# Sliding attention: outputs by feature and turned back, or by query at once

## The reference

```
s = einsum('bcqhgd,bckhd->bchgqk', qc, kb) * (HEAD_DIM ** -0.5)
s = where(kmask, s + bias, -inf)
p = softmax(concatenate([s, sink], axis=-1), axis=-1)[..., :-1]
o = einsum('bchgqk,bckhd->bcqhgd', p, vb)
```

## Time and profile before

| | us |
|---|---|
| median of 3 runs | 2401.78 |
| the runs | 2395.17, 2401.78, 2403.42 |
| span of the profiled execution, first to last instruction | 2401.4 |
| TensorE busy, records | 2179.5 (91%), 11296 |
| VectorE busy | 1648.4 (69%) |
| ScalarE busy | 1486.0 (62%) |

### The profile page before, as it was taken

The page is one execution under the profiler, slowest core; times in us unless marked ns, Lnnn a source line. Parts: engine busy times, 40 slices in busy tenths (PEclk is TensorE's granted clock), DMA queues, the critical chain, the costliest instruction groups (busy, mean ns, idle before and its releaser), DMA issues. The chain is left out here.

```text
span 2401.4 us, 35987 instructions
## 1 busy us (share of the span) xinstructions
PE 2179.5 (91%) x11296; PEld 1794.5 (75%) x11296; DVE 1648.4 (69%) x3068; ACT 1486.0 (62%) x2262; POOL 467.5 (19%) x529
## 2 busy tenths in 40 slices
PE   6999999879789999999899984999999999999980
PEld 5788888756477877877678873778888888788860
DVE  5323231267587777777733346999999999999976
ACT  4323241276587777777633331878887888788867
POOL 0111111143122222221000001222222222122221
PEclk9999999979989999999899995999999999999995
DMA  6535352543441222222233325997887969998838
GB/s 202 175 116 181 114 185 86 154 91 93 114 109 51 58 71 69 64 69 77 56 122 140 141 95 184 350 370 238 298 266 228 299 199 364 317 299 300 266 91 301
DMA packets 220554, 420.62 MB, mean 175 GB/s; under 512 B 47912, under 2 KB 97144, under 8 KB 219288
## 3 DMA queue, kind: packets, MB, share of 16 engines
q1 hardware_dynamic: 187760, 316.08, 39.1%
q0 software_dynamic: 31648, 101.89, 14.7%
q10 hardware_dynamic: 1040, 1.31, 0.2%
HBM read 437.68 MB, written 86.39 MB: 218 GB/s over the span
## 5 line engine op out<-in xcount | busy, mean ns | idle before, releaser
L2533 DVE TENSOR_TENSOR moe_w_lo<-fetch_w_raw,moe_w_hi 128x1024 fp32r<-128x1024 f32 x376 | 435.2, 1217 | 8.8 <-ACT moe_w_hi L2462 8.6
L2462 ACT ACTIVATE moe_w_hi<-fetch_w_raw 128x1024 fp32r<-128x1024 f32 x376 | 368.8, 1053 | 60.6 <-PEq L96 27.9
L2587 PE MATMUL moe_ps_gu<-moe_w_hi,moe_xT_hi 128*128 128x512 f32 x736 | 294.1, 400 | 4.0 <-DVE moe_xT_lo L2544 4.0
L2589 PE MATMUL moe_ps_gu<-moe_w_hi,moe_xT_lo 128*128 128x512 f32 x736 | 289.3, 393 | 0.0
L2588 PE MATMUL moe_ps_gu<-moe_w_lo,moe_xT_hi 128*128 128x512 f32 x736 | 289.1, 393 | 0.0
L1495 ACT ACTIVATE fox_p_hi<-fox_ps_t 128x512 fp32r<-128x512 f32 (+4 forms) x352 | 182.4, 533 | 102.2 <-PE fox_ps_t L1635 100.6
L1562 DVE TENSOR_TENSOR fox_p_lo<-fox_ps_t,fox_p_hi 128x512 fp32r<-128x512 f32 (+4 forms) x352 | 211.6, 613 | 47.4 <-ACT fox_p_hi L1495 45.6
L2539 DVE TENSOR_TENSOR moe_d_lo<-fetch_d_raw,moe_d_hi 128x1024 fp32r<-128x1024 f32 x184 | 213.1, 1220 | 10.9 <-ACT moe_d_hi L2470 10.9
L1635 PE MATMUL fox_ps_t<-ident,fox_s 128*128 128x128 f32 (+1 forms) x1216 | 198.1, 278 | 18.2 <-ACT fox_s L1488 17.9
L1549 DVE CUSTOM_DVE_ANT_0 fox_s<-fox_ps_r,fox_ncum 128x512 f32<-128x512 f32 (+4 forms) x352 | 191.7, 570 | 22.9 <-PE fox_ps_r L1620 16.0
L511 ACT ACTIVATE proj_qk_out<-proj_ps_chunk 128x512 f32<-128x512 f32 x52 | 31.1, 598 | 261.7 <-PE proj_ps_chunk L744 261.7
(11 more groups left out here) (346 smaller groups left out, 5061.1 us busy)
## 6 DMA issues: line engine op xcount, KB each, us to landing
fetch_w_raw<-in_w_e_gate_dram SPq DMA_DIRECT2D x192, 512.0 KB
fetch_w_raw<-in_w_e_up_dram SPq DMA_DIRECT2D x192, 512.0 KB
fetch_d_raw<-in_w_e_down_dram SPq DMA_DIRECT2D x92, 1024.0 KB
ahead_raw<-in_w_in_dram SPq DMA_DIRECT2D x24, 1024.0 KB, 5.2
gates_wide<-in_x_dram SPq DMA_DIRECT2D x16, 512.0 KB
h<-gates_wide POOLq DMA_DIRECT2D x16, 512.0 KB, 3.3
gates_wide<-qT SPq DMA_DIRECT2D x32, 256.0 KB, 4.4
mix_h<-h SPq DMA_DIRECT2D x16, 512.0 KB, 3.6
```

Of the source, the lines that this page charges most:

```text
L2462: nc.scalar.activation(w_hi[:, k], w_raw[:, k].rearrange("p j n -> p (j n)"), ACT.Copy).then_inc(gu_high, 1)
L2533: nc.vector.tensor_tensor(w_lo[:, k], w_raw[:, k].rearrange("p j n -> p (j n)"), w_hi[:, k].bitcast(F32), ALU.subtract).then_inc(gu_split, 1)
L2587: nc.tensor.matmul(out, xT_hi[:, slot, k], w_hi[:, k, cols], start=k == 0, stop=False)
L2589: done = nc.tensor.matmul(out, xT_lo[:, slot, k], w_hi[:, k, cols], start=False, stop=k == KT - 1)
```

## The change

The value products change sides. For each of the four heads of a kv the turned probabilities of that head (80 or 128 keys by 128 queries) are the stationary operand, and the 65 value columns are moving. The result is 128 queries by 65 columns, four heads side by side in the same bank, 260 columns in all. `copy_outputs`, `turn_back`, the tile `oT`, its zeroing and the semaphores between them go. `divide` waits for the products (`pv_used`) and reads PSUM with a step of 65 columns between heads instead of 128.

```diff
--- before.py
+++ after.py
@@ -860,7 +860,6 @@
         esink = m.sb("esink", [P, 3, A_HEADS])
         inv = m.sb("inv", [P, 3, A_HEADS])
         pT = m.sb("pT", [P, 2, 4, 4 * P])
-        oT = m.sb("oT", [P, A_KV, 4 * P])
         o = m.sb("o", [P, 2, A_HEADS * HD])
         forget, b_forget, one = gates["forget"], gates["b_forget"], gates["one"]
         fa = m.sb("fa", [B_HEADS, TOK])
@@ -871,7 +870,6 @@
         fstep = m.sem("fstep")
         dstep = m.sem("dstep")
         cum_stored = m.pool_dma_sem("cum_stored")
-        zeroed = m.sem("zeroed")
         fox_zeroed = m.sem("fox_zeroed")
         k_in = ahead["win_k_in"]
         k_high = m.sem("k_high")
@@ -892,8 +890,6 @@
         pv_used = m.sem("pv_used")
         summed = m.sem("summed")
         inverse = m.sem("inverse")
-        oT_out = m.sem("oT_out")
-        o_turned = m.sem("o_turned")
         o_ready = m.sem("o_ready")
         o_stored = [m.pool_dma_sem(f"o_stored{i}") for i in range(2)]
         block = ctx.enter_context(nc.Block())
@@ -1001,12 +997,6 @@
                 nc.scalar.activation(pT[:, n % 2, 2 * kv + 1], ps_pT[(4 * n + 2 * kv + 1) % T_BANKS][:], ACT.Copy
                                      ).then_inc(pT_act, 1)
 
-            def copy_outputs(n, kv):
-                act.wait_ge(pv_used, 2 * n + kv + 1)
-                wait(act, o_turned, 2 * (n - 1) + kv + 1)
-                nc.scalar.activation(oT[0:HD + 1, kv], ps_o[kv][0:HD + 1], ACT.Copy).then_inc(oT_out, 1)
-
-            act.wait_ge(zeroed, 1)
             queries_high(0)
             keys_high(0)
             queries_high(1)
@@ -1026,22 +1016,17 @@
                 for half in range(2):
                     if is_tile(n - 1):
                         exponentials(n - 1, half)
-                    if half == 0 and is_tile(n - 3):
-                        copy_outputs(n - 3, 1)
                     if is_tile(n - 2):
                         copy_turned(n - 2, half)
                 if is_tile(n - 1):
                     sink_exponentials(n - 1)
                 if is_tile(n + 2):
                     queries_high(n + 2)
-                if is_tile(n - 2):
-                    copy_outputs(n - 2, 0)
 
             rounds(body)
 
         @block.vector
         def _(dve):
-            nc.vector.memset(oT[:], 0.0).then_inc(zeroed, 1)
             def keys_low(quad):
                 dve.wait_ge(k_high, 4 * (quad + 1))
                 for kv in range(A_KV):
@@ -1082,14 +1067,15 @@
                 if kv == 0:
                     dve.wait_ge(sink_exp, n + 1)
                     wait(dve, o_stored[n % 2], 16 * (n // 2))
-                dve.wait_ge(o_turned, 2 * n + kv + 1)
-                total = ps_o[kv][:].rearrange("p (h d) -> p h d", d=P)[:, :, HD:HD + 1].squeeze(2)
+                dve.wait_ge(pv_used, 2 * n + kv + 1)
+                out = ps_o[kv][:, 0:4 * (HD + 1)].rearrange("p (h d) -> p h d", d=HD + 1)
+                total = out[:, :, HD:HD + 1].squeeze(2)
                 nc.vector.tensor_tensor(inv[:, n % 3, heads], total, esink[:, n % 3, heads], ALU.add).then_inc(summed, 1)
                 dve.wait_ge(summed, 2 * n + kv + 1)
                 nc.vector.reciprocal(inv[:, n % 3, heads], inv[:, n % 3, heads]).then_inc(inverse, 1)
                 dve.wait_ge(inverse, 2 * n + kv + 1)
                 nc.vector.tensor_tensor(o[:, n % 2].rearrange("p (h d) -> p h d", d=HD)[:, heads],
-                                        ps_o[kv][:].rearrange("p (h d) -> p h d", d=P)[:, :, 0:HD],
+                                        out[:, :, 0:HD],
                                         inv[:, n % 3, heads].unsqueeze(2).to_broadcast([P, 4, HD]),
                                         ALU.mult).then_inc(o_ready, 1)
 
@@ -1171,18 +1157,13 @@
                 wait(pe, o_ready, 2 * (n - 1) + kv + 1)
                 pe.wait_ge(pT_dve, 2 * n + kv + 1)
                 pe.wait_ge(pT_act, 2 * n + kv + 1)
-                out = ps_o[kv][0:HD + 1]
-                nc.tensor.matmul(out, v_prev[0:PREV, slot, kv], pT[0:PREV, turned, 2 * kv], start=True, stop=False)
-                nc.tensor.matmul(out, v_cur[:, slot, kv], pT[:, turned, 2 * kv + 1], start=False, stop=True
-                                 ).then_inc(pv_used, 1)
-
-            def turn_back(n, kv):
-                pe.wait_ge(oT_out, 2 * n + kv + 1)
                 for j in range(4):
-                    done = nc.tensor.transpose(ps_o[kv][:, j * P:(j + 1) * P], oT[:, kv, j * P:(j + 1) * P], ident[:])
-                done.then_inc(o_turned, 1)
-
-            pe.wait_ge(zeroed, 1)
+                    out, queries = ps_o[kv][:, j * (HD + 1):(j + 1) * (HD + 1)], slice(j * P, (j + 1) * P)
+                    nc.tensor.matmul(out, pT[0:PREV, turned, 2 * kv, queries], v_prev[0:PREV, slot, kv],
+                                     start=True, stop=False)
+                    done = nc.tensor.matmul(out, pT[:, turned, 2 * kv + 1, queries], v_cur[:, slot, kv],
+                                            start=False, stop=True)
+                done.then_inc(pv_used, 1)
 
             def body(n):
                 if is_tile(n):
@@ -1192,15 +1173,11 @@
                 if is_tile(n):
                     scores(n, 1)
                     scores(n, 2)
-                if is_tile(n - 3):
-                    turn_back(n - 3, 0)
                 if is_tile(n - 2):
                     turn(n - 2, 0)
                     turn(n - 2, 1)
                 if is_tile(n):
                     scores(n, 3)
-                if is_tile(n - 3):
-                    turn_back(n - 3, 1)
                 if is_tile(n - 2):
                     turn(n - 2, 2)
                     values(n - 2, 0)
```

## The result

The changed kernel takes 2412.22 us (median of 4 runs, 2410.70 to 2414.34) against 2402.25 before: ratio 1.0048, 95% interval 1.0034 to 1.0063. It is slower by about 10 us, where 2397 was forecast. The profiled execution took 2411.32 us with a span of 2409.7, 8.3 above the span before.

The account below looks back on a forecast made before the run. The prediction took a loop through TensorE, ScalarE and VectorE, 8.87 us a round, as the bound. From 2401.8 us, -1.9 - 0.4 - 2.5 = -4.8 gave 2397 us, range 2390 to 2426 with rivals (its own 2391 to 2405).

Parts of the forecast that it names:

- rounds 7 to 15: Nine even rounds: division waits saved, -1.8 us, against start cost of the loads, +1.4; together -0.4 (bounds -3 and +3).
- The case in which the clock falls: Rival: TensorE drops to 1.2 GHz in this stage; four rounds at half clock, +24 - 5, 2421 us; chance 0.30.
- Decides from round 5: Where the half-clock rival sets in: the clock is down there and the dense value products no longer bring it back.
- Value products: Each value call: 16 load and matmul pairs at 0.107 us plus 0.08 at the start, 1.79 us (bounds 1.60 and 1.95).
- Turn backs in VectorE's shadow: Even rounds: removing 8 transposes a tile wins only VectorE's 0.19 us wait, as TensorE then waits about 1.1 us.
- Division: VectorE's division: same three instructions, PSUM step 65 instead of 128, unchanged at 0.42 us (0.40 to 0.45).
- Zeroing: Stage start: dropping the 0.91 us memset is worth 0 (bounds -0.9 and 0), as ScalarE then waits for keys.
- Rounds 3 to 6: Rounds where ScalarE also does forget gates and its output copies are late: -1.9 us (bounds -3.7 and 0).
- The end: Last rounds, without scores: copies and last division start earlier without turn backs, -2.5 us (bounds -3.2 and -1.5).
- The rival in which TensorE bounds at full clock: Rival: the loop is TensorE's own work, so each of 16 tiles wins 0.88 us: 2386 us; chance 0.08.
- loads cheaper than 0.107: Rival: a load and matmul pair takes 0.08 us, each call 0.43 us shorter: 2387 us; chance 0.04.
- that nothing moves: Rival: the loop is held elsewhere, so the time stays at 2402 us; chance 0.03.

Follow-up runs that it names:

- e9: The changed kernel itself, unaltered, run again beside the filler kernel on one chip as its base: 2413.56 us (1.0058 of the kernel before).
- e1: The changed kernel with 128 moving columns instead of 65 in each value product, the extra results never read: 2395.53 us (0.9979 of the kernel before).
- e4: The changed kernel with 128 moving columns, VectorE's first turned copy before its third bias, TensorE's second scores before values 1: 2381.17 us (0.9915).
- e6: The changed kernel with its 65 columns, VectorE's first turned copy before its third bias, TensorE's second scores before values 1: 2398.73 us (0.9976).
- e8: The changed kernel plus one unused 512-column product ahead of each value call of key head 0, in the wait for VectorE's copy: 2403.16 us (1.0007).
- e5: The kernel before, value products untouched, with VectorE's first turned copy before its third bias and TensorE's second scores before values 1: 2394.81 us (0.9967).

## Why the forecast was wrong

The direction was missed, and one step did most of it: *rounds 7 to 15*, put at -0.4 us (bounds -3 and +3) with the clock at 1.00 from 543 us. Those bounds held only the loop's durations. From values 0 of the sixth tile (552.02 after, 556.11 before) to those of the fourteenth (633.71 and 628.29) the change loses 9.5 us; from there to the last division it loses another 1.8, where -2.5 was forecast, with the clock at 0.75. In the profile of e9, the changed kernel again, these two parts lose 10.7 and 6.5 us (values 0 at 555.99 and 638.84, division at 666.67). The case in which the clock falls stood beside it as a rival, with its cause (65 columns a load, waits of 1.2 and 0.6 us, measured 0.95 and 0.35) and with 0.30; it is what happened. e1 against the changed kernel and e4 against e6 show the columns as the cause, and e8 fits. Its chance was too low: the rows that it weighed showed the fall behind a single wait of 1.41 us, and the counter-evidence (short waits that cost no clock) came from rounds with 512-column products, which the change removes.

The size within the rival: I took four rounds at +6.0, 2421. Measured, the rounds with a spell take 11.77, 12.10 and 12.14 us (from 579.73, 600.62 and 621.57), about 3.2 us over 8.8 each, and the rest comes in the last rounds. The price of +6.0 took a whole round at half clock with all of TensorE's work in it; a spell lasts some 9 us and starts 2 us or more into its round, where it also swallows the waits. Then full clock returns for a round. "Decides from round 5" differs from run to run: here the clock was at 1.00 from 536 to 582, and rounds with and without a spell alternate after it; in e9 the spells begin before 575.

The other steps, with e1 as the change at full clock:
- *Value products*, 16 pairs at 0.107 and 0.08 at the start, 1.79 us a call: measured 1.77 and 1.80. The sum is right, its two terms are off and cancel: a pair takes 0.112 (12 of them from 574.37 to 575.71), and the start costs some 0.02 (the first two pairs 0.24 for 0.22). The two streams of the earlier trace rows did not both give 0.107: the 8 pairs in 1.10 us give 0.118 each, and the 0.08 was put in to make up for it. A pair takes as long with 128 moving columns as with 65 (e1), so it is not the 65 columns that set its time. At the rate of the 512-column records (0.44 us each) 128 columns take 0.11 us themselves, by this estimate; more than 128 were not tried. The 81 ns a pair of the Trainium skill ("TensorE: Matmul & The Clock Gate", Back-to-back issue gap) is not what fp32 gives here: 0.112.
- *Turn backs in VectorE's shadow*, 0.19 us a round: right within 0.1 us. The round is 8.80 to 8.83 us against 8.87, waits of 0.95 us (1.1 forecast), and e5 shows them on the path once the shadow is gone.
- *Division* 0.42 us and no wait in the even rounds: right. *Zeroing* worth nothing: the first value call starts at 504.62, no earlier than the 503.81 of before; e5, which has the zeroing, has 504.66.
- *Rounds 3 to 6*, -1.9 (bounds -3.7 and 0): the last value call of this part was forecast at 537.9 and came at 537.64, for 541.11 before. The 1.2 us that I took off for a clock that comes back just past 540 were not lost: -3.6 at the fifth tile (e1 -3.4), the lower bound's case. But this agreement is luck. The forecast had TensorE wait 3.9 us at full clock until 532.9 and fall behind that. In the profile of the changed kernel the clock falls at 524 already, behind a wait of 0.95 us; TensorE works at 1.2 GHz without a wait until 534.52, while ScalarE is busy with the gates, and is back at full clock from there. The fall was cheap here because TensorE would have waited anyway: e1, with the same stretch at full clock, waits 3.06 us there, until 533.45, and falls behind that wait (0.78 in 534 to 536, 0.50 in 536 to 538), which is the way the forecast had it.
- *The end*, -2.5 (bounds -3.2 and -1.5): +1.8 in the changed kernel, as said. e1 goes from the fourteenth tile's values 0 (627.13) to its last division (646.66) in 19.53 us, before takes 21.37 (from 628.29): -1.8.
- *The rounds between* in e1: 44.18 us for five against 44.35: -0.03 each, -0.3 over nine, next to the -0.4.

By these, without a spell, it is -3.4 - 0.3 - 1.8 = -5.5, beside the -4.8 of the sum. e1 measured -5.7 by its medians. Its profile, with one spell of 2.8 us (a round of 11.66 us instead of 8.87), has the last division only 3.0 us earlier than before; another 3.4 us of its shorter span lie behind the stage, where the scatter is. So the loop's durations were sized well, which the stage's own times show better than the -5.7, and the clock on which they rested was not there. The forecast's own range was written as 2391 to 2405; its bounds add up to 2391 and 2403, which changes nothing here.

The rival in which TensorE bounds at full clock (2386) fell with the waits of 0.95 us; loads cheaper than 0.107 fell with the pair; that nothing moves fell with the trace.

## What to carry to other kernels

A change that swaps few wide products for many narrow ones must be priced at both clocks: when the weight load sets the pace, TensorE looks as busy as before, but moves fewer columns in the same time, and may drop to 1.2 GHz. If the pace is the load's, pad the moving operand up to what costs next to nothing behind it (here 128 columns, with a neighbour's data and results nobody reads). And take waits out before or with such a change: the turn backs it removes were worth nothing in the shadow of VectorE, and the padded change as a whole some 12 us once the two orders were mended. Without the padding (e6, 0.9976) it was no better than the old form with the same orders (e5, 0.9967).

## What the runs showed of the hardware

- An fp32 pair of 128-column load and matmul takes 0.11 us with 65 and with 128 moving columns (values 0: 1.80 and 1.85 us a call; the 0.05 lies at the start), and 0.21 at half clock (call of 3.41 us): load and matmul both follow the granted clock.
- More TensorE work made a kernel faster (e8: 16 more products, 10 us less; e1: twice the columns, some 16 us less).
- PE busy alone doesn't tell whether the clock holds: 5.70 of 7 us busy before it fell in the changed kernel, 21.73 of 25 and 23.48 of 28 in e1 where it held, 24.54 of 25 and 26.16 of 28 in e6, at 1.00 and 0.88.
- The runs of e6 lie 19 us apart, those of the other eight kernels of the experiments 5 to 12, and those of the kernel before 7 to 13.
